# mLSTM steps of a hybrid trunk: transposes three halves and values five halves behind the scores

## The reference, cut to what matters

```python
Dlog = bcum[..., :, None] - bcum[..., None, :] + ig[..., None, :]
Dlog = jnp.where(tri, Dlog, -jnp.inf)
m_t = jnp.maximum(inter_log, jnp.max(Dlog, axis=-1))
Dw = jnp.exp(Dlog - m_t[..., None])
sqk = jnp.einsum('bhcld,bhcsd->bhcls', qc, kc) * Dw
num = ... + jnp.einsum('bhcls,bhcse->bhcle', sqk, vc)
den = ... + jnp.sum(sqk, axis=-1)
h = num / jnp.maximum(jnp.abs(den), jnp.exp(-m_t))[..., None]
...
hm = hm * lax.rsqrt(jnp.mean(hm * hm, axis=-1, keepdims=True) + EPS)
y_ml = (hm * jax.nn.sigmoid(mo.astype(jnp.float32))).astype(h.dtype)
```

## Time and profile before

| | us |
|---|---|
| median of 3 runs | 966.34 |
| lowest, highest | 964.74, 966.46 |
| profiled execution, its own time | 965.01 |
| its span, first to last instruction | 963.3 |
| PE busy | 938.5 (97%) |
| DVE busy | 550.1 (57%) |
| ACT busy | 400.9 (42%) |
| GpSimd busy | 14.1 (1%) |

### The profile page before, as it was taken

How to read it: one execution, slowest core, us unless ns; L and a number is a source line. 1 busy time by engine, 2 the same in 40 slices (tenths; PEclk the granted TensorE clock), 3 DMA queues, 4 the chain that set the end, 5 groups by cost and what they waited for, 6 DMA issues and landing times.

```text
span 963.3 us, 11714 instructions
## 1 busy us (share of the span) xinstructions
PE 938.5 (97%) x4605; PEld 762.0 (79%) x4605; DVE 550.1 (57%) x967; ACT 400.9 (42%) x648; POOL 14.1 (1%) x38
## 2 busy tenths in 40 slices
PE   7999999999998999999999999999999999999996
PEld 6778777777776878889978768888888888888885
DVE  5632667333456662768333533848957875885535
ACT  4431455344424323335434532455535545634511
POOL 4000000000000000000000000000000000000000
PEclk9999999999999999999999999999999999999999
DMA  8311220222112162442521243120441261063202
GB/s 284 117 46 61 88 88 19 71 88 88 44 45 88 42 227 84 142 140 77 208 88 37 95 143 119 45 81 8 137 170 44 78 225 48 1 199 107 87 1 88
DMA packets 44814, 92.61 MB, mean 96 GB/s; under 512 B 1772, under 2 KB 1864, under 8 KB 44760
## 3 DMA queue, kind: packets, MB, share of 16 engines
q1 hardware_dynamic: 43192, 86.54, 26.5%
q0 software_dynamic: 1568, 5.32, 1.7%
HBM read 89.76 MB, written 2.10 MB: 95 GB/s over the span
## 4 chain that ended last, share of the span: by engine, by line
PE 87%; DVE 7%; ACT 3%; issue 1%; DMA 1%; SPq 0%; DVEq 0%; ACTq 0%
PE bank L1267 64%; PE bank L1298 12%; DVE w_lo L926 2%; PE bank L1471 1%; PE bank L1422 1%; DVE conv_acc L1012 1%; PE bank L1311 1%; PE bank L1365 1%; ACT w_hi L706 1%; PE bank L1409 1%; PE bank L1392 1%; PE bank L1377 1%; PE bank L1449 1%; PE bank L1436 1%; DMA stage<-in_w_in 1%
## 5 line engine op out<-in xcount | busy, mean ns | idle before, releaser
L926 DVE TENSOR_TENSOR w_lo<-stage,w_hi 128x1024 fp32r<-128x1024 f32 x174 | 205.1, 1220 | 91.5 <-ACT w_hi L706 91.4
L1267 PE MATMUL bank<-act_hi,w_hi 128*128 128x512 f32 (+2 forms) x624 | 246.3, 395 | 2.2 <-DVE act_lo L1092 2.2
L1267 PE MATMUL bank<-act_hi,w_lo 128*128 128x512 f32 (+2 forms) x624 | 241.1, 386 | 0.0
L1267 PE MATMUL bank<-act_lo,w_hi 128*128 128x512 f32 (+2 forms) x624 | 240.8, 386 | 0.0
L706 ACT ACTIVATE w_hi<-stage 128x1024 fp32r<-128x1024 f32 x174 | 174.6, 1052 | 129.6 <-PE bank L1267 67.6
L1267 PEld LDWEIGHTS bank<-act_hi,w_hi 128*128 128x128 f32 x624 | 117.9, 189 | 24.4 <-issue 2.4
L1267 PEld LDWEIGHTS bank<-act_hi,w_lo 128*128 128x128 f32 x624 | 117.5, 188 | 24.0
L1267 PEld LDWEIGHTS bank<-act_lo,w_hi 128*128 128x128 f32 x624 | 117.8, 189 | 22.0
L1267 PE MATMUL bank<-w_hi,act_hi 128*128 128x512 f32 x256 | 101.5, 397 | 5.2 <-DVE w_lo L926 2.7
L1267 PE MATMUL bank<-w_hi,act_lo 128*128 128x512 f32 x256 | 99.8, 390 | 0.0
L1267 PE MATMUL bank<-w_lo,act_hi 128*128 128x512 f32 x256 | 99.7, 389 | 0.0
(11 more groups left out here) (250 smaller groups left out, 1255.2 us busy)
## 6 DMA issues: line engine op xcount, KB each, us to landing
stage<-in_w_in SPq DMA_DIRECT2D x20, 1024.0 KB, 4.9
stage<-in_w_mlp_in SPq DMA_DIRECT2D x16, 1024.0 KB, 5.2
stage<-in_w_mlp_out SPq DMA_DIRECT2D x16, 1024.0 KB, 5.5
stage<-in_w_xkv SPq DMA_DIRECT2D x8, 1024.0 KB, 4.9
stage<-in_w_mix_out SPq DMA_DIRECT2D x4, 1024.0 KB, 5.0
stage<-in_w_xq SPq DMA_DIRECT2D x4, 1024.0 KB, 5.1
stage<-in_w_xo SPq DMA_DIRECT2D x4, 1024.0 KB, 5.0
x_tok<-in_x SPq DMA_DIRECT2D x4, 512.0 KB, 9.9
```

Source lines behind the costliest of these rows:

```text
L926: dve.tensor_tensor(w_lo[:, r:r + 2, :], stage_pair(pair), w_hi[:, r:r + 2, :].bitcast(F32), ALU.subtract).then_inc(s_low, 1)
L1267: ins = pe.matmul(dst, still[q], moving[q], start=(k == 0 and q == 0), stop=(k == nk - 1 and q == 2))
```

## The change

Transposes and their copies go from two to three halves behind the scores, values from four to five, and all steps of a finished head one half later with them. `prob` and `prob_b` are used as four buffers in turn, and DVE's wait before it overwrites one is put back from the task two before to the task four before.

```diff
@@ make_steps
     for t in range(X0):
-        before(place[t] + 4, ("values", t))
+        before(place[t] + 5, ("values", t))
     for t in range(X0):
-        before(place[t] + 2, ("turn", t))
+        before(place[t] + 3, ("turn", t))
     for t in range(X0):
         before(place[t], ("scores", t))
         after(place[t], ("probs", t))
     for t in range(X0):
-        after(place[t] + 2, ("turned", t))
+        after(place[t] + 3, ("turned", t))
...
     for h in range(ML_HEADS):
-        w = place[NT * h + NT - 1] + 4
+        w = place[NT * h + NT - 1] + 5
         after(w, ("ml_quotient", h))
         after(w + 1, ("ml_squares", h))
         after(w + 2, ("ml_norm", h))
@@ trunk
+        def ml_prob(t):
+            return (prob, prob_b)[t % 4 // 2][:, t % 2, :]
...
-                    if n >= 2:
-                        dve.wait_ge(s_pturn, n - 1)
-                    dve.tensor_tensor_reduce(prob[:, i2, 0:keys], bank[5][:, 0:keys], dwt[:, 0:keys],
+                    if n >= 4:
+                        dve.wait_ge(s_pturn, n - 3)
+                    dve.tensor_tensor_reduce(ml_prob(n)[:, 0:keys], bank[5][:, 0:keys], dwt[:, 0:keys],
...
-                    keys, src, dst = task(t)[2], prob[:, t % 2, :], bank[4]
+                    keys, src, dst = task(t)[2], ml_prob(t), bank[4]
```

## The result

| | before | after |
|---|---|---|
| median, us | 966.34 | 969.87 |
| lowest, highest | 964.74, 966.52 | 968.39, 970.43 |
| ratio, 95% interval | | 1.0041 (1.0026 to 1.0055) |
| span of the profiled execution | 963.3 | 968.1 |

The changed kernel is slower by 0.4%, 3.5 us. The median lies in the range I gave (965.2 to 970.5), 1.6 us over my value. In the changed kernel the lines of the code are three further down: L1436 is now L1439, L1449 is L1452, L1456 is L1459, L1267 is L1270, L1199 is L1202.

The account below looks back on a forecast made before the run. TensorE, busy 938.5 of 963.3 us, was taken as the bound, so only its pauses could change. Terms -1.2 +0.1 +2.0 +1.0 were summed to +2.0 us, giving 968.3 us from the median; range 965.2 to 970.5.

Parts of the forecast that it names:

- (1): Probability buffers: the wait moved from n-1 to n-3 transposes never held anything, so removing it gives 0 us.
- (3): Halves 59 to 70: no pause; 0.1 us for the scores of task 2, which lose the transposes before them.
- (4): Halves 71 to 74: new pauses of 2.5 and 0.5 us in place of 4.15; 1.2 us won.
- (5): Tail, halves 79 to 84: head 3's head transposes pause 3.1 us, not 1.1; half 84 newly pauses 1.0.
- Rival C: Pause of 3.1 us ahead of half 83 lowers TensorE's clock: +5.5 us on the +2.0, 973.8 us; chance 0.04.
- A: Covered tail: one of the two tail pauses is not there, 966.2 to 967.2 us; chance 0.25.
- B: Longer distance helps: waits of the transposes go in halves 72 and 73, faster, 962.8 us; chance 0.08.
- D: Later knock-on: w_lo pair 46 and 47 pushed back, half 86 waits another 0.3 to 1.5 us; chance 0.13.

Follow-up runs that it names:

- experiment 1: Kernel before with only the four probability buffers and the wait put back to the task four before, all places unchanged: 965.83 against 966.65 us, ratio 1.0003.
- (2): Kernel before with ScalarE's copy to prob_t ahead of the exponential in each half: 966.18 against 966.65 us, ratio 1.0004.
- 5, gate_early: Changed kernel with each head's gating ahead of weight splits and take in its half: 967.98 us, ratio 1.0008 to before.
- experiment 6, norm_early: Changed kernel with squares and norm of head 3 one half earlier: 970.32 us, ratio 1.0046 to before.
- 8 to 11: Weight pairs 40, 41, 44, 45 split later: in before 965.66 us; in changed kernel 969.31; there with gating and head 3's norm early 965.02, with 44, 45 after half 82 962.37.
- after_again: The changed kernel run once more, nothing altered: 970.32 against 966.48 us for before, ratio 1.0037.
- fill_first: Changed kernel with 18 idle transposes of the identity filling only the pause ahead of the values of task 8: 970.59 us, ratio 1.0035 to before.
- gate_norm_early: Changed kernel with gating ahead of weight splits and take, and head 3's squares and norm one half earlier: 967.28 us, ratio 1.0005 to before.
- splits_late_after: Changed kernel with weight pairs 40, 41 split after half 75 and 44, 45 after half 83: 969.31 us, ratio 1.0030 to before.
- fill_both: Changed kernel with idle transposes filling the pauses ahead of task 8's values (18) and head 3's head transposes (23): 968.82 us, ratio 1.0017 to before.

## Why the prediction was right, and where it was not

The direction held, and the mechanism of the pauses: the wait on the buffers held nothing (experiment 1), the transposes' own waits were no gain (2), and the time is set by where the heads' steps meet the weight splits on DVE (5, 6, 8 to 11). That the median lies in the range owes something to luck: the range was made without the clock, and the clock is what took the time to its upper end.

**(1) Buffers, 0 us.** Right.

**(3) Halves 59 to 70, 0.1 us.** Nothing is to be seen there: the scores of task 11 end at 287.25, against 288.33 in before, where 0.89 us of values and 0.22 of transposes more had been done by then.

**(4) Halves 71 to 74.** The wait of task 8's values was put at 2.5 us and is 2.3, for the reason given. The second pause, 0.5, isn't in the profiled execution. In it half 72 ran at the lower clock, 1.5 us longer, so DVE had caught up; with the clock up there is 0.2 ahead of the transposes (L1439) in the changed kernel run again, 0.3 with the first pause filled. My 4.15 us of pauses in before are what is left when the work is taken off; the list of waits has only 2.8 there (2.6 and 0.2), since it counts a pause from the modelled end of the matmul before, and the first piece behind a pause is longer (0.46 us and not 0.22 for the two matmuls at 297.31). Counted in the way of the 4.15, the execution of after has 2.5 us of pauses and 1.7 of clock (from 287.25 to the start of half 75 at 314.82 are 27.57 us, with 23.4 of work in them), and the changed kernel run again, whose clock stays up, 3.1 us of pauses, where 2.9 were forecast.

**(5) The tail.** The wait for ml_h was put at 3.1 and is 2.9; that of half 84 at 1.0 and is 0.9. The cause given for the first was shown by late splits.

**The sum.** +2.0 us was forecast from pauses (the terms as written add up to 1.9). In the execution whose clock stays up the change costs +2.2: 1.0 won in halves 70 to 74, where 1.2 was forecast, and 3.3 lost in the tail, where 3.0 was. The sum was right. The +1.3 to +1.4 of the means are less, because in executions with a stretch at the lower clock part of the later pauses is hidden behind it.

**Rival C, the clock: the step that failed.** It stood at a chance of 0.04, for the pause of 3.1 alone, with a price of 5.5 us. It happened: on the mean of the executions at 1.4 us, in the profiled one twice, at 1.7 us each, behind the 2.3 us pause as well. I took the clock of before to be full everywhere but at the end, because every slice of the page shows a 9. That was a misreading: a 9 is 90% or more, and before itself has a stretch at 0.50 at 87 us (last section). And I reasoned from one pause of 2.56 us in one execution that left the clock up. That row was an outcome of that execution, not a bound: in the profiled execution with both pauses filled the same early pause, 2.6 us, is followed by a clock of 0.50 from 17 to 21 us. The price per stretch, on the other hand, was three times too high, from supposing that both halves 83 and 84 run at half speed. With 1.4 us of clock in the mean the sum would have been +3.4, or 969.7, against 969.87 measured; that this is so near is chance, since the means differ by 2.7 us and only the medians by 3.5. The Trainium skill, "TensorE: Matmul & The Clock Gate", section "Why this matters for your kernels", warned of idle gaps in the middle of a kernel; this case bears it out for gaps of 2.3 and 2.9 us, but not in every execution: over all profiled executions, five of ten unfilled pauses of 2.2 to 2.9 us in this part of the kernel are followed by a stretch at 0.50, and none of the shorter or filled ones is.

**A** (covered tail) did not occur. **B** is refuted by the result itself, where the waits of the transposes went and the time rose, and by experiment 2. **D**: no wait of half 86 is in after; it appears only when the splits are later still.

Open: why some executions lose clock behind the same pause. The traces do differ before it. Of the 14 profiled executions, over all kernels, seven have a stretch at 0.50 at 11 to 14 us; the other seven have none there, but one (in two of them a double one) that begins at 87 to 89 us, and three of them one at 17 us as well. Five of the ten long pauses fall in executions of the first kind (after_again, fill_first, gate_norm_early, splits_late_after), and none of them is followed by a stretch; the other five fall in executions of the second kind (after, gate_early, norm_early), and all are. fill_both is of the second kind and stays at 1.00 in both filled places, which speaks for the fillers; fill_first is of the first kind, so its profile says nothing about the clock. That something early in an execution decides is an inference from seven executions with such pauses; no experiment tests it.

## What to carry to other kernels

A step moved in a hand-written order is priced by its new neighbours in the in-order queues: list, for every moved step, what stands ahead of it on its engine afterwards, with takes that free a bank among them (experiment 6 is what comes of leaving one out). Before lengthening a distance in a pipeline, see whether its wait is the last to end; if the queue of one engine is what is late, take work out of the crowded halves, which, with the gating and the last norm moved forward, brought 4.2 us in the median here (2.8 at full clock), where four buffers brought none. Price a new TensorE pause of 2 us or more with the chance of a stretch at the lower clock behind it, and compare kernels also with that loss taken out, best between two executions whose clock stays up over the part that was changed.

## What the runs showed of the hardware that I had not expected

A stretch at the lower clock loses 1.7 us of clock (3.4 where two follow each other, as at 300 us in the kernel of experiment 6), but what it costs depends on where it falls. At 87 us it costs 1.6 us: without it half 59 starts at 236.60 in the kernel of experiment 1, whose steps up to there are those of before, and with it at 238.17. At 11 us it costs nothing, since PE waits for w_lo right behind it. This is the changed kernel run again, a window and a line of PE's timeline:

```profile
11.00:12.00 1.00, 1.00 (x3) 0.76 (x3) 1.00 (x2) 1.00 (x3) 1.00 (x2) 0.50 1.05 408
...
16.75 0.47 PE L1270 MATMUL bank<-w_hi,act_hi 128*128 128x512 f32 x1 [1.40 <-DVE w_lo L929]
```

In before, with the clock up there, the same matmul starts at 16.86, behind a wait of 2.56. Behind the pause at 295 us a stretch costs 1.05 of its 1.7 us: from the start of half 70 to that of half 75 are 27.5 us with it and 26.5 without. Executions of one kernel differ by steps of this size: on the second chip before comes at 964.8, 966.4 and 968.1, with little between. The stretches aren't all behind pauses. In the profiled execution of before there is one at 87 us, where PE is fully busy (windows):

```profile
86.00:87.00 1.00, 1.00 (x12) 1.00 (x11) 0.42 (x1) 0.00 (x0) 0.00 (x0) 1.00 0.00 0
...
88.00:89.00 1.00, 1.00 (x4) 0.72 (x3) 0.15 (x1) 0.00 (x0) 0.00 (x0) 0.50 0.00 0
```

What it did before, in its timeline, were matmuls of 12 columns:

```profile
86.42 0.82 PE L1345 MATMUL bank<-forget,ones 128*128 128x12 f32 x6
87.09 0.57 PE L1345 MATMUL bank<-forget,upto 128*128 128x12 f32 x2
```

The sums over the forget gates (L1342, L1345) run from 84.2 us with 12 columns each; after them the clock is at 0.50 for the next projection. That they are the cause was not tested; the seven executions with the stretch at 11 us run the same matmuls at 1.00.
